# Keys and values of a fixed memory made at the start of a decoder layer, spilled and reloaded for the cross-attention

## The reference

```python
u = rms_norm(x, g_mix)
z = u @ w_in                      # MLA latents, retention q/k/v/gate, two branch gates
h = x + (sigmoid(gA) * MLA(z) + sigmoid(gR) * Retention(z)) @ w_out
xq  = (rms_norm(h, g_cross) @ w_xq).reshape(S, 4, 256)
mkv = (rms_norm(mem, g_mem) @ w_xkv).reshape(M, 2, 4, 256)      # mem: 256 x 1024
mk, mv = mkv[:, 0], mkv[:, 1]
p = softmax(einsum('shd,mhd->hsm', xq, mk) * 256 ** -0.5)
h = h + einsum('hsm,mhd->shd', p, mv).reshape(S, D) @ w_xo
h = h + w_down(silu(a) * b)       # a, b = causal_dwconv3(rms_norm(h, g_ffn) @ w_up)
out = rms_norm(h, g_final)
```

## Time and profile before

| | us |
|---|---|
| median of 2 runs (2056.86 to 2060.11) | 2058.49 |
| the profiled execution | 2060.93 |
| its span | 2059.1 |
| granted TensorE clock, mean | 0.972 |
| PE, DVE, ACT, POOL busy | 1926.0, 920.7, 557.6, 844.3 |
| first dense block starts | 36.21 |
| last cross query ends, first scores start | 1071, 1133.76 |

### The profile page before, as it was taken

One profiled execution on the slowest core, in us unless ns is written; L12 is line 12 of the kernel. 1 busy time (PEld: TensorE's weight loads), 2 busy tenths in 40 slices (PEclk: granted clock), 3 DMA queues, 4 the chain that ended last, 5 costly groups with the idle time before them and its releaser, 6 DMA issues.

```text
span 2059.1 us, 25536 instructions
## 1 busy us (share of the span) xinstructions
PE 1926.0 (94%) x9308; PEld 1605.1 (78%) x9308; DVE 920.7 (45%) x1522; ACT 557.6 (27%) x988; POOL 844.3 (41%) x324
## 2 busy tenths in 40 slices
PE   5999999999978888899999889999999999999997
PEld 4888888888767776778778778787888788878876
DVE  5454540000166666453431543666146516741664
ACT  5222231100245555211223421422022202210223
POOL 4333334566320001244326134455655564555451
PEclk9999999999979999999999999999999999999998
DMA  4111112233110002532114112111211121112112
GB/s 152 42 31 31 35 47 92 82 95 107 43 31 1 1 1 66 194 120 102 42 41 134 51 49 84 42 51 51 62 51 51 51 62 51 47 55 62 51 48 85
DMA packets 35339, 128.39 MB, mean 62 GB/s; under 512 B 4032, under 2 KB 4160, under 8 KB 35264
## 3 DMA queue, kind: packets, MB, share of 16 engines
q1 hardware_dynamic: 25776, 92.72, 14.9%
q10 hardware_dynamic: 9488, 34.61, 4.4%
HBM read 110.54 MB, written 16.78 MB: 62 GB/s over the span
## 4 chain that ended last, share of the span: by engine, by line
PE 76%; DVE 9%; issue 6%; ACT 5%; DMA 2%; POOL 1%; SPq 0%; ACTq 0%; DVEq 0%; POOLq 0%
PE ps L309 23%; PE ps L314 23%; PE ps L315 23%; PE ps L588 3%; POOL wl L284 1%; ACT prow L1016 1%; PE ps L567 1%; ACT pr L1177 1%; DVE p1l L1268 1%; DVE t L1271 1%; DVE amax L1541 1%; DMA xs<-in_x 1%; DVE ul L1271 1%; DVE yb L1775 1%; PE ps L383 0%
## 5 line engine op out<-in xcount | busy, mean ns | idle before, releaser
L291 POOL TENSOR_SCALAR wh<-raw 128x1024 fp32r<-128x1024 f32 x152 | 429.9, 2828 | 1105.5 <-PE ps L309 910.0
L293 POOL TENSOR_TENSOR wl<-raw,wh 128x1024 fp32r<-128x1024 f32 x152 | 376.3, 2475 | 12.7
L309 PE MATMUL ps<-uh,wh 128*128 128x512 f32 (+1 forms) x576 | 229.3, 398 | 3.3 <-DVE ul L1271 3.3
L315 PE MATMUL ps<-uh,wl 128*128 128x512 f32 (+1 forms) x576 | 226.3, 393 | 0.0
L314 PE MATMUL ps<-ul,wh 128*128 128x512 f32 (+1 forms) x576 | 226.2, 393 | 0.0
L309 PE MATMUL ps<-fah,wh 128*128 128x512 f32 x352 | 139.5, 396 | 9.0 <-DVE fal L1268 6.6
L315 PE MATMUL ps<-fah,wl 128*128 128x512 f32 x352 | 138.4, 393 | 0.0
L314 PE MATMUL ps<-fal,wh 128*128 128x512 f32 x352 | 138.4, 393 | 0.0
L309 PE MATMUL ps<-f0h,wh 128*128 128x512 f32 x352 | 137.0, 389 | 1.3 <-DVE z L1759 1.3
L309 PE MATMUL ps<-f1h,wh 128*128 128x512 f32 x352 | 137.7, 391 | 0.3 <-DVE f1l L1271 0.3
L315 PE MATMUL ps<-f1h,wl 128*128 128x512 f32 x352 | 137.7, 391 | 0.0
(11 more groups left out here) (347 smaller groups left out, 4128.2 us busy)
## 6 DMA issues: line engine op xcount, KB each, us to landing
raw<-in_slabs SPq DMA_DIRECT2D x168, 512.0 KB, 3.6
xs<-in_x SPq DMA_DIRECT2D x8, 512.0 KB, 7.6
s_ga<-sig ACTq DMA_DIRECT2D x8, 512.0 KB, 2.6
s_mr<-mxr ACTq DMA_DIRECT2D x8, 512.0 KB, 5.0
xtile<-in_x ACTq DMA_DIRECT2D x8, 512.0 KB, 6.1
sab<-s_ga ACTq DMA_DIRECT2D x8, 512.0 KB, 4.2
mrb<-s_mr ACTq DMA_DIRECT2D x8, 512.0 KB, 5.2
s_h<-hT ACTq DMA_DIRECT2D x8, 512.0 KB, 2.6
```

Of the source, the lines that this page charges most:

```text
L291: pool.tensor_scalar(wh[:, j, :], raw[:, j % RAWS, :], 1.0, None, ALU.mult).then_inc(S["w_hi"], 1)
L293: pool.tensor_tensor(wl[:, j, :], raw[:, j % RAWS, :], wh[:, j, :].bitcast(f32), ALU.subtract).then_inc(S["w_ready"], 1)
L309: l = pe.matmul(o, lh, rh, start=start, stop=False)
L315: return pe.matmul(o, ll, rh, start=False, stop=stop)
```

## The change

The memory comes first. At the start SP loads its rows, then the small tables, then the eight key slabs, all into a buffer of their own (`rawk`), with the first three row tiles of x between them, then value slabs and the rest of x. Keys are made as before, 8 blocks; values directly in rows, with the memory as the stationary operand and the weights moving, 512 columns at a time, so nothing is turned back. For that a value slab is gathered by the DMA from four stored slabs (two blocks of 128 rows each), in pieces of 1 KB, and its blocks are put in another order by the access patterns of the upper part and of the subtraction (`by_row`, `out_row`). Between the value blocks TensorE turns x, two tiles of 512 columns at a time, in four banks instead of six; VectorE makes the angle steps between the key remainders. The first retention block waits for the tiles of u one by one, and for the banks of the last values.

`mkh` and `mkl` are spilled to memory from ScalarE's queue after value block 5, `mvh` and `mvl` after the sines (1 MB each). The waits for the spill stand before VectorE's first rotation and ScalarE's first `kr_hi`. The reloads go by head, three DMAs each (`head_kv`): heads 0 and 1 when the root mean square is copied (`rb_c`), before the query copies; heads 2 and 3 after the second step of cross-attention, into places of their own. The two loads of `hs` move behind the first step. Some semaphores are shared by stages that follow one another.

The numbers of the first uses and slabs, and SP's order:

```diff
+SLAB0, FF_SLAB0 = starts((("xkv", 2 * KB), ("ret", 4 * RH), ("ga", KB), ("gr", 2 * KB), ("lat", 4), ("mla", 4), ("mix", KB // 2),
+                          ("out", KB), ("xq", KB), ("xo", KB)))
+USE0, FF_USE0 = starts((("xk", KB // 2), ("xv", 1), ("ret", 4 * RH), ("ga", KB), ...
...
+            def value_slab(s):
+
+                c, i = divmod(s - KB, SLOTS)
+                m = DRAM_XKV + KB + CH * c
+                sp.dma_start(raw[:, s % RAWS, :].rearrange("p (m n) -> p m n", m=CH),
+                             slabs[m:m + CH, :, 2 * i * P:2 * (i + 1) * P].rearrange("m p n -> p m n")).then_inc(
+                    S[f"ld{s % RAWS}"], 16)
+            for r in range(MB):
+                sp.dma_start(mrow[:, r, :], mem[r * P:(r + 1) * P, :]).then_inc(S["mm_ld"], 16)
+            sp.dma_start(cn[:, :], const).then_inc(S["par"], 16)
+            sp.dma_start(sm[:, :], small).then_inc(S["par"], 16)
+            sp.dma_start(posi[:, :], pos).then_inc(S["par"], 16)
+            for i in range(KB // 2):
+                sp.dma_start(rawk[:, 2 * i:2 * i + 2, :], slabs[DRAM_XKV + 2 * i:DRAM_XKV + 2 * i + 2].rearrange("s p n -> p s n")).then_inc(S[f"ld_k{i}"], 16)
+                if i:
+                    sp.dma_start(xs[:, i - 1, :], x[(i - 1) * P:i * P, :]).then_inc(S[f"x_ld{i - 1}"], 16)
+            for j in range(RAWS):
+                value_slab(KB + j)
+            for t in range(3, NT):
                 sp.dma_start(xs[:, t, :], x[t * P:(t + 1) * P, :]).then_inc(S[f"x_ld{t}"], 16)
```

TensorE at the start, and the first dense block:

```diff
+            def key_block(m):
+                b = m % 2
+                pe.wait_ge(S["w_ready"], m + 1)
+                at_least(pe, d_free[b], m // 2)
+                for k in range(KB):
+                    if m == 0:
+                        pe.wait_ge(S["mm_lo"], k + 1)
+                    l = mm3(ps[:, b, 0:NMEM], *wslot(m % SLOTS, k), mth[:, k, :], mtl[:, k, :], k == 0, k == KB - 1,
+                            freed=int(k == 0 and m > 0))
+                l.then_inc(d_done[b], 1)
...
+            def value_rows(c, i):
+                pe.wait_ge(S["w_ready"], KB + SLOTS * c + i + 1)
+                if c == 1 and i == 0:
+                    for b in range(2):
+                        pe.wait_ge(d_free[b], USE0["xv"])
+                for r in range(MB):
+                    for k in range(2):
+                        rows = slice(r * P, (r + 1) * P)
+                        l = mm3(ps[:, r if c else 2 + r, :], mth[:, 2 * i + k, rows], mtl[:, 2 * i + k, rows],
+                                *wslot(i, k, H2), i == k == 0, i == SLOTS - 1 and k == 1, freed=int(r == k == 0))
+                    if i == SLOTS - 1:
+                        l.then_inc(d_done[r] if c else S["v_done"], 1)
...
+            for m in range(KB):
+                key_block(m)
+            for i in range(2 * SLOTS):
+                value_rows(i // SLOTS, i % SLOTS)
+                turn_x(2 * i)
+                turn_x(2 * i + 1)
...
-            pe.wait_ge(S["xT_lo"], 2 * KB)
+            def u_ready(k, b):
+                pe.wait_ge(S["xT_lo"], KB * b + k + 1)
```

ScalarE at the start:

```diff
+            for s in range(RAWS):
+                slab_hi(s)
+            for k in range(KB):
+                act.wait_ge(S["mm_t"], k // 2 + 1)
+                c = (k % 2) * NMEM
+                copy(mth[:, k, :], ps[:, 4 + k // 2, c:c + NMEM], scale=smc("g_mem", k)).then_inc(S["mm_hi"], 1)
+            for m in range(KB):
+                slab_hi(m + RAWS)
+                if m >= 2:
+                    x_square(m - 2)
+                act.wait_ge(d_done[m % 2], m // 2 + 1)
+                copy(mkh[:, m, :], ps[:, m % 2, 0:NMEM]).then_inc(S["kv_h"], 1)
+            x_square(KB - 2)
+            x_square(KB - 1)
+            for i in range(2 * SLOTS):
+                if KB + RAWS + i < 2 * KB:
+                    slab_hi(KB + RAWS + i)
+                x_hi(2 * i)
+                x_hi(2 * i + 1)
+                if i == SLOTS:
+                    for r in range(MB):
+                        value_hi(0, r)
+                if i == SLOTS + 1:
+                    for b in range(2):
+                        act.wait_ge(d_free[b], USE0["xv"])
+                    act.dma_start(s_k[0], mkh[:, :, :].bitcast(f32)).then_inc(S["kv_sp"], 16)
+                    act.dma_start(s_k[1], mkl[:, :, :].bitcast(f32)).then_inc(S["kv_sp"], 16)
+            for r in range(MB):
+                value_hi(1, r)
```

VectorE at the start:

```diff
+            for n in range(4):
+                angle(n)
+            dve.wait_ge(S["mm_st"], 1)
...
+            for m in range(KB):
+                dve.wait_ge(S["kv_h"], m + 1)
+                l = lo(mkl[:, m, :], ps[:, m % 2, 0:NMEM], mkh[:, m, :])
+                l.then_inc(d_free[m % 2], 1)
+                if m < 6:
+                    angle(4 + m)
+                if m == KB - 2:
+                    x_rows(0)
+            for i in range(2 * SLOTS):
+                x_lo(2 * i)
+                x_lo(2 * i + 1)
+                if i == 1:
+                    x_rows(1)
+                if i == SLOTS:
+                    for r in range(MB):
+                        value_lo(0, r)
+            for r in range(MB):
+                value_lo(1, r)
```

The reload and its places in ScalarE's queue:

```diff
+            def head_kv(j):
+                k, v = (kj0, kj1, kj2, kj3)[j], (vj0, vj1, vj2, vj3)[j]
+                act.dma_start(k[:, :, :, :].bitcast(f32), s_k[:, :, 2 * j:2 * j + 2, :].rearrange("l p c n -> p l c n")).then_inc(
+                    S[f"kv_ld{j % 2}"], 16)
+                act.dma_start(v[:, 0, :, :].bitcast(f32), s_v[0, :, :, j * XD:(j + 1) * XD]).then_inc(S[f"kv_ld{j % 2}"], 16)
+                act.dma_start(v[:, 1, :, :].bitcast(f32), s_v[1, :, :, j * XD:(j + 1) * XD]).then_inc(S[f"kv_ld{j % 2}"], 16)
+            act.wait_ge(S["rb_c"], 1)
+            for j in range(2):
+                head_kv(j)
...
+                if v == 1:
+                    for j in (2, 3):
+                        head_kv(j)
+                if v == 0:
+                    for m in range(2):
+                        act.dma_start(hs[:, m, :], s_h[m]).then_inc(S[f"hs_ld{m}"], 16)
```

More of the change, by code:

```diff
@@ new lines, in _ @@
+            for j in range(RAWS):
+                value_slab(KB + j)
+            for t in range(3, NT):
+                sp.dma_start(xs[:, t, :], x[t * P:(t + 1) * P, :]).then_inc(S[f"x_ld{t}"], 16)
+            for s in range(KB + RAWS, 2 * KB):
+                sp.wait_ge(S["w_ready"], s - RAWS + 1)
+                value_slab(s)
+            for a, b, back in ((2 * KB, SLAB0["xo"], 2 * KB), (SLAB0["xo"], NSLAB, 0)):
+                with sp.Fori(a // SLOTS, b // SLOTS) as i:
+                    for j in range(SLOTS):
+                        sp.wait_ge(S["w_ready"], SLOTS * i + (j - RAWS + 1))
+                        sp.dma_start(raw[:, j % RAWS, :], row(slabs, SLOTS * i + (j - back))).then_inc(
+                            S[f"ld{j % RAWS}"], 16)
@@ L294, in split @@
                                    ALU.subtract).then_inc(S["w_ready"], 1)
[L295 to L301, removed]
+            for s in range(SLAB0["ret"]):
+                split(s // SLOTS, s % SLOTS, 0, False)
+            with pool.Fori(SLAB0["ret"] // SLOTS, NSLAB // SLOTS) as i:
+                for j in range(SLOTS):
+                    split(i, j, SLAB0["ret"])
         @block.tensor
@@ L1190, in _ @@
             xa_exp(0)
-            v_turned(KB - 1)
-            for m in range(2):
-                act.dma_start(hs[:, m, :], s_h[m]).then_inc(S[f"hs_ld{m}"], 16)
             for v in range(2 * XH):
@@ L1286, in _, with x_lo @@
                         S["x_row"], 1)
-            for n in range(2 * KB):
+            def x_lo(n):
                 b, k = n // KB, n % KB
                 dve.wait_ge(S["xT_hi"], n + 1)
-                stt(ul[:, k, half(b)], ps[:, 2 + n % 6, :], smc("g_mix", k), uh[:, k, half(b)].bitcast(f32), ALU.mult,
+                stt(ul[:, k, half(b)], ps[:, 4 + n % 4, :], smc("g_mix", k), uh[:, k, half(b)].bitcast(f32), ALU.mult,
                     ALU.subtract).then_inc(S["xT_lo"], 1)
-            step = [0]
```

321 lines of the change are left out of this document (143 added, 178 removed).

## The result

The changed kernel takes 2031.62 us, median of 2 runs (2029.77 to 2033.46), against 2058.49: a ratio of 0.9879 (95% interval 0.9848 to 0.991). The medians are 26.9 us apart, and the ratio is worth 24.9 us of 2058.49, so the gain is 25 to 27 us. Its profiled execution spans 2031.6 us, against 2059.1.

What follows compares the result with a forecast made beforehand. TensorE, busy 94% of the span, was taken as the bound, so moved work gains only in its idle time. Span 2059.1 + 38.8 - 64.1 = 2033.8, median forecast 2033 us, range 2026 to 2046.

Steps and rivals of the forecast that it cites:

- The middle: Cross-attention: scores wait only for the last query remainder, 60.3 us less; first transposes gain 3.8 more; sum 64.1.
- The front: Start of the kernel, with the memory work moved there: first dense block at 75.0 instead of 36.2, 38.8 us more.
- Two row scalings at 6.39 / 4 = 1.6 us: At the start, VectorE scales the memory's rows at 1.6 us each, ending at 14.5.
- 1.3: In the front, TensorE waits 1.3 us for VectorE's scalings before the first transpose of x.
- 1.2: Among the value blocks, 1.2 us of waiting for value slabs, which have two buffers only.
- TensorE alone sets the front: Case from below: value slabs no slower and the rest meshes, so TensorE's own work paces the front; 2031.
- Late value slabs: Rival in the front: landings in 1 KB pieces take twice 3.6 us, adding 11 us: 2044; chance 0.14.
- Ports: Rival in the front: each VectorE scaling of x waits out a GpSimd subtraction, 10 to 18 us: 2043 to 2051; chance 0.08.
- Clock: Rival in the front: TensorE stays at 1.2 GHz because of small waits, 50 us more: 2083; chance 0.04.
- Its half-speed stretch after the wait exists before as well: First dense block: runs partly at half speed after its wait, as before the change, so no difference.
- Edits at nothing: Angle steps, table load and sines, spill, later spill waits and reloads of heads: nothing on the path.
- so nothing; without the cover 2.7: Query stage: six reload issues for heads 0 and 1, 2.7 us, hidden by a half block of 5.5; uncovered 2.7.

Runs made afterwards that it cites:

- ref: The changed kernel run again, unaltered: 2031.23 us, ratio 0.988 to the kernel before.
- contiguous: Changed kernel with value slabs stored in order of use, one 4 KB piece a row instead of four of 1 KB: 2034.42 us, ratio 0.9885.
- two_products: Changed kernel with two products instead of three for the values (memory's remainder times weights' upper part left out): 2037.59 us, ratio 0.9898.
- reload_later: Changed kernel with heads 0 and 1 reloaded behind the first two query blocks instead of before them: 2029.8 us, ratio 0.9868.
- angles_late: Changed kernel with six of the ten angle steps moved behind the last value remainder: 2033.06 us, ratio 0.9867.
- shared_place: Changed kernel with heads 2 and 3 reloaded into the places of 0 and 1, each when its place is free: 2047.26 us, ratio 0.9937.
- best: Changed kernel, GpSimd's first subtraction after the memory's row scalings, heads 0 and 1 reloaded behind second query block, key spill behind sines: 2026.53 us, ratio 0.9853.
- ref_again: The changed kernel run once more, unaltered, in the last group: 2031.31 us, ratio 0.9879 to the kernel before.
- spill_wait: Changed kernel with ScalarE waiting for the spill right behind its issue: 2032.51 us, ratio 0.9886.

## Why the prediction was right

| step | predicted | profile after |
|---|---|---|
| small tables used | 7.9 | 7.87 |
| four angle steps done | 11.3 | 10.6 |
| memory's rows scaled | 14.5 | 16.4 |
| key block 0 ends | 20.5 | 23.0 |
| key block 7 ends | 40.7 | 43.2 |
| values end | 72.9 | 72.8 |
| first dense block | 75.0 | 75.23 |
| middle: scores; transposes | -60.3; -3.8 | -60.2; -3.8 |
| first eight transposes there | as before | +0.5 |
| reload issues, heads 0 and 1 | 0 | +1.8 |
| half clock in the first dense block | as before | -2.8 |
| span | 2033.8 | 2031.6 |

**The middle** was right in kind and size. The scores waited for nothing but the last query remainder. They then ran partly at half clock (0.57 from 1112 to 1116) behind a wait of 2.4 us, as the keys in the earlier trace rows did behind one of 3.97. The first transposes start at 1121.98 against 1146.93, which is the predicted 3.8 on top of the 60.2. The eight of them then take 1.55 us against 1.03, behind a wait of 2.00 and at a granted 0.62 (from 1122 to 1124); this 0.5 is what the first copy of `xph` is late. The 2 us that the prediction left in its range for such waits held it.

**The front** came out by 0.2 us, but by two errors that cancel. "Two row scalings at 6.39 / 4 = 1.6 us" was mis-sized: 5.65 for the two, 2.4 more, in this execution (3.5 in ref). The row was a mean over scalings of 0.75, 1.52 and 2.83, and the two here both met a subtraction. Everything behind followed within 0.6 of its predicted distance, at 2.88 a key block. Then "1.3" of waiting for the scaled x and "1.2" for slabs were 0.3 and nothing, 2.2 less. That 2.4 too little and 2.2 too much nearly cancel was luck.

**"TensorE alone sets the front"**, given only as the case from below, is what happened after 20 us; but the experiments add that it is no more than level with the chain through VectorE, ScalarE, GpSimd and the slabs. Taking 31 us of matmuls away gave 1.6.

**Late value slabs**: 3.3 on the chain against the 7.2 that the rival needed; contiguous excludes it. The landing of 7.16 that did occur, in two_products, was of a slab in pieces of 4 KB, beside a spill, a collision that the prediction doesn't have.

**Ports**: the mechanism is right, and both reasons that I gave against it were misreadings. "So a full wait each time doesn't show" was a reading of a mean, and "The trace has that case" was not so: of GpSimd's three instructions beside that row one was a subtraction. The rival was wrong in turn to charge every scaling. Five of ten met a subtraction, and on the path the price was 4.2 us at most, for the two scalings of the memory's rows, not 10 to 18: the eight of x lie under TensorE's work, which waited 0.3 us for them.

**Clock**: the granted clock is 1.00 through the whole front. The sixteen transposes at its head still took 0.23 us each (3.61 / 16), close to the 0.22 predicted from those of the kernel before, where those of the middle took 0.12; the matmuls follow each other at 0.12 from 19.81 on. "Its half-speed stretch after the wait exists before as well" was wrong for this execution, which had none (-2.8). Behind the same wait of 2.4 us ref, reload_later, contiguous, angles_late, shared_place and best had one (in ref the first copy came 7.4 us behind the block's start, not 5.7), ref_again and spill_wait had none. It comes and goes, and I can't say by what.

**Edits at nothing**: angles, the wait for the spill and the reload of heads 2 and 3, each tested or read in the trace, nothing. The reload of heads 0 and 1, "so nothing; without the cover 2.7", was mis-sized: 1.7. The issues took 3.6 us in all, not six times 0.45, and held ScalarE's first copy, VectorE's product with it, and both banks; the wait of 1.4 came twice. My own upper bound held it.

What stays open: the 3.2 us in the stages that the change doesn't touch. They are of the size by which the profiled executions of one and the same kernel differ (2028.3 to 2031.6), so of the 27.5 us in the spans only 24.3 are traced to the change; the ratios, at 24.7 to 24.9 us, leave room for that.

## What to carry to other kernels

Work that depends on nothing can be moved to where an engine starves, but its gain is the time that goes at the old place less the time that comes at the new: here 63.6 less 39.0. Both were predicted within 0.6 us from the trace of before, the second with some luck. A moved reload is free only with a place of its own and a gap to be issued in; ahead of the first instruction of a stage six issues cost 1.7 us. And don't take the mean of a row where VectorE works beside GpSimd: look for the single durations under it and for what GpSimd did in that row, and put the few instructions at the head of the whole chain where the other engine is quiet.

## What the runs showed of the hardware

A VectorE scaling of 128 x 1024 float32 takes 0.75 us, or 2.8 to 2.95 beside a subtraction of GpSimd; beside GpSimd's pass that makes an upper part it took 0.75 or 1.52 (kernel before), and once 1.01 (ref_again). Which of them it is changes from execution to execution of one kernel. A load of 512 KB takes 3.3 us in pieces of 1 KB and no less in pieces of 4 KB (3.46 in contiguous), and up to 7.16 beside a spill of 2 MB on another queue. And 7.4 us less work for TensorE gave nothing: it waited 6.8 us instead of 2.4 for its first dense block and 4.0 instead of 0.3 before it, and ran 4 us behind the wait at 1.2 GHz.
